# Two adjoining blocks on one core: the modulation chunks of the linear attention's input stage are computed behind its later projections, and the context and the small parameters are loaded later

## The reference, cut to what matters

```python
def modulate(h, shift, scale):
    return h * (1 + scale[:, None]) + shift[:, None]
...
    proj = h @ w_in
    q, k, v, g, a_lr = jnp.split(
        proj, [GLA_QK, 2 * GLA_QK, 2 * GLA_QK + GLA_VD, 2 * GLA_QK + 2 * GLA_VD], axis=-1)
    log_a = jax.nn.log_sigmoid((a_lr @ w_gate_up + b_gate).astype(jnp.float32)) / GLA_GATE_TAU
```

## Time and profile before

| | us |
|---|---|
| median of 3 runs | 1647.23 (1647.05 to 1648.43) |
| the profiled execution's own time | 1646.89 |
| span of its trace, first to last instruction | 1645.1 |
| PE busy (share of the span) | 1586.4 (96%) |
| DVE busy | 1025.4 (62%) |
| ACT busy | 650.4 (40%) |

### The profile page before, as it was taken

The page is one execution under the profiler, slowest core; times in us unless marked ns, Lnnn a source line. Parts: engine busy times, 40 slices in busy tenths (PEclk is TensorE's granted clock), DMA queues, the critical chain, the costliest instruction groups (busy, mean ns, idle before and its releaser), DMA issues.

```text
span 1645.1 us, 24028 instructions
## 1 busy us (share of the span) xinstructions
PE 1586.4 (96%) x9719; PEld 1235.1 (75%) x9719; DVE 1025.4 (62%) x1597; ACT 650.4 (40%) x925; POOL 0.2 (0%) x4
## 2 busy tenths in 40 slices
PE   6999899999999998999999999999999999999998
PEld 3788656766787875567677868977647788999998
DVE  3647654423795476454337968449857664689886
ACT  3444323322573442323236662424234342254443
POOL 0000000000000000000000000000000000000000
PEclk9999999999999998999999999999999999999999
DMA  9966798888998598888989973325622333645540
GB/s 350 304 227 218 259 358 339 335 322 329 360 346 279 188 317 325 306 342 311 349 327 359 342 235 101 104 77 204 229 79 79 105 124 119 214 137 197 179 155 26
DMA packets 188245, 393.12 MB, mean 239 GB/s; under 512 B 11365, under 2 KB 102232, under 8 KB 174824
## 3 DMA queue, kind: packets, MB, share of 16 engines
q1 hardware_dynamic: 186462, 390.21, 66.3%
q10 hardware_dynamic: 1674, 1.38, 0.3%
HBM read 390.52 MB, written 1.05 MB: 238 GB/s over the span
## 4 chain that ended last, share of the span: by engine, by line
PE 82%; DVE 8%; DMA 6%; ACT 2%; issue 1%; ACTq 0%; SPq 0%; DVEq 0%
PE bank L716 10%; PE bank L1129 8%; PE bank L1689 8%; PE bank L1156 4%; PE bank L1432 4%; PE bank L1192 4%; PE bank L1142 4%; PE bank L1700 4%; PE bank L1225 3%; PE bank L743 3%; PE bank L760 3%; DMA ring<-in_moe_w_up_dram 3%; PE bank L1210 2%; PE bank L807 2%; PE bank L776 2%; PE bank L911 2%
## 5 line engine op out<-in xcount | busy, mean ns | idle before, releaser
L2673 DVE TENSOR_TENSOR parts<-ring,parts 128x2048 fp32r<-128x2048 f32 x84 | 191.6, 2290 | 166.6 <-ACT parts L1998 166.0
L1787 ACT ACTIVATE work<-bank 128x256 f32<-128x256 f32 (+3 forms) x227 | 98.8, 447 | 378.1 <-PE bank L716 58.1
L1998 ACT ACTIVATE parts<-ring 128x2048 fp32r<-128x2048 f32 x84 | 160.5, 1921 | 150.9 <-DMA ring<-in_moe_w_up_dram 48.9
L716 PE MATMUL bank<-hh,ring 128*128 128x256 f32 x640 | 141.5, 380 | 2.3 <-ACT work L1787 1.8
L716 PEld LDWEIGHTS bank<-hh,ring 128*128 128x128 f32 x640 | 120.4, 190 | 21.6 <-issue 5.8
L1129 PE MATMUL bank<-parts 128*128 128x512 f32 x576 | 132.5, 391 | 0.0
L1689 PE MATMUL bank<-parts 128*128 128x256 f32 x1056 | 128.6, 283 | 1.4 <-DVE parts L3306 1.4
L1689 PEld LDWEIGHTS bank<-parts 128*128 128x128 f32 x1056 | 127.6, 192 | 2.2 <-issue 2.2
L1129 PEld LDWEIGHTS bank<-parts 128*128 128x128 f32 x576 | 107.7, 188 | 27.1 <-issue 4.9
L1156 PE MATMUL bank<-ring,work 128*64 128x512 f32 x512 | 113.6, 595 | 4.1 <-DMA ring<-in_moe_w_up_dram 4.1
L3262 DVE TENSOR_TENSOR parts<-ring,parts 128x2048 fp32r<-128x2048 f32 x37 | 84.8, 2292 | 16.2 <-ACT parts L2307 15.6
(11 more groups left out here) (379 smaller groups left out, 2709.6 us busy)
## 6 DMA issues: line engine op xcount, KB each, us to landing
ring<-in_moe_w_gate_dram SPq DMA_DIRECT2D x64, 1024.0 KB, 9.1
ring<-in_moe_w_up_dram SPq DMA_DIRECT2D x64, 1024.0 KB, 5.8
ring<-in_moe_w_down_dram SPq DMA_DIRECT2D x64, 1024.0 KB, 9.5
ring<-in_ada_w_dram SPq DMA_DIRECT2D x48, 1024.0 KB, 8.6
ring<-in_w_in_dram SPq DMA_DIRECT2D x32, 1024.0 KB, 5.9
ring<-in_w_mod_dram SPq DMA_DIRECT2D x24, 1024.0 KB, 7.5
ring<-in_w_up_dram SPq DMA_DIRECT2D x22, 1024.0 KB, 5.2
ring<-in_gla_w_in_dram SPq DMA_DIRECT2D x12, 1024.0 KB, 8.5
```

The costliest lines, as they stand in the source:

```text
L716: ins = pe.matmul(ps[:, 0:n], w[:, k, m * P:(m + 1) * P], rhs(k), start=k == 0, stop=k == kt - 1)
L1787: act.activation(dst, view, func, **kw).then_inc(tiles.taken, 1)
L1998: act.activation(moe_w[:, i % 3, 0, :], ring[:, g % RING, :], ACT.Identity)\
L2673: dve.tensor_tensor(moe_w[:, i % 3, 1, :], ring[:, (MOE_AT[layer] + AT[n, kind, half, 0]) % RING, :], moe_w[:, i % 3, 0, :].bitcast(F32), ...
```

## The change

Projections 0 to 3 are loaded and computed one behind the other; chunks 4 to 7 move behind projections 4, 5, 6 and 7. Chunks 4, 5 and 6 are turned behind projections 5, 6 and 7, chunk 7 behind projection 8. ACT's copies and DVE's reductions move with them. In SP's list slots 8 to 12 are projections 0 to 4, 13 and 14 chunk 4, 15 projection 5, 16 and 17 chunk 5, 18 projection 6, 19 and 20 chunk 6, 21 projection 7, 22 and 23 chunk 7, 24 projection 8; from 24 on the list is as before. The context is loaded ahead of slot 12, and the small parameters ahead of slots 13 to 24, four each.

```diff
--- before.py
+++ after.py
@@ -115,7 +115,7 @@
 MOD_CHUNKS = 12
 RING = 6
 FRONT = (2, 3, 0, 1)
-WITH_GLA_IN = {0: (0, 4), 1: (0, 5), 4: (0, 6), 5: (0, 7)}
+WITH_GLA_IN = {4: (0, 4), 5: (0, 5), 6: (0, 6), 7: (0, 7)}
 BEFORE_GLA_OUT = [(0, i) for i in range(8, 11)]
 WITH_ROUTER = [[(0, 11)] + [(1, i) for i in range(4)], [(1, 10), (1, 11)] + [(2, i) for i in range(4)]]
 SHARED = 8
@@ -635,7 +635,7 @@
             loads.append((d_skip[64 * (hd % 2):64 * (hd % 2) + 64, hd // 2:hd // 2 + 1],
                           A["s_d_2"][0, hd:hd + 1].rearrange("(n o) -> n o", o=1).to_broadcast([64, 1])))
         n_params = 16 * len(loads)
-        PARAMS_FROM, PARAMS_EACH = 9, 3
+        CTX_AT, PARAMS_FROM, PARAMS_EACH = 12, 13, 4

         def ring_half(n, b, of=ring):

@@ -936,24 +936,16 @@
                 ps = to_dve.fill(pe)
                 close(to_dve, pe.matmul(ps[:, 0:T], w_gate_up[:, m * P:(m + 1) * P], g_lr[0:16, :],
                                         start=True, stop=True))
-            mod_chunk(*WITH_GLA_IN[0])
-            in_linear(to_act, gla_parts)
-            mod_turn(4)
-            mod_chunk(*WITH_GLA_IN[1])
-            in_linear(to_act, gla_parts)
-            mod_turn(5)
-            in_linear(to_act, gla_parts)
+            for _ in range(3):
+                in_linear(to_act, gla_parts)
             pe.wait_ge(sem("ctx_landed"), 16)
             input_turned(c_in, "ctx_turned")
-            in_by_token(to_act, gla_parts)
-            mod_chunk(*WITH_GLA_IN[4])
-            in_by_token(to_act, gla_parts)
-            mod_turn(6)
-            mod_chunk(*WITH_GLA_IN[5])
-            in_by_token(to_act, gla_parts)
-            mod_turn(7)
-            in_by_token(to_act, gla_parts)
-            values_in = to_act.n
+            for j in range(4, 8):
+                in_by_token(to_act, gla_parts)
+                values_in = to_act.n
+                if j > 4:
+                    mod_turn(j - 1)
+                mod_chunk(*WITH_GLA_IN[j])
             pe.wait_ge(sem("gla_kdec"), 1)
             for t in range(TT):
                 ps = to_dve.fill(pe)
@@ -962,6 +954,7 @@
                 close(to_dve, ins)
             keys_in = to_dve.n
             in_linear(to_act, gla_parts)
+            mod_turn(7)
             norm_sum([sq[:, k, T:TC] for k in range(KT)], T)
             pe.wait_ge(to_dve.taken, keys_in)
             pe.wait_ge(to_act.taken, values_in)
@@ -1738,7 +1731,7 @@
             experts_at = {}
             sp.wait_ge(sem("cleared"), 1)
             for g, (what, arg) in enumerate(SLOTS):
-                if g == PARAMS_FROM - 1:
+                if g == CTX_AT:
                     sp.dma_start(c_in, A["ctx_2"][0].rearrange("(t p) n -> p t n", p=P)).then_inc(sem("ctx_landed"), 16)
                 at = PARAMS_EACH * max(g - PARAMS_FROM, 0)
                 for to, src in loads[at:at + PARAMS_EACH] if g >= PARAMS_FROM else ():
@@ -1920,7 +1913,6 @@
             for j in range(2):
                 take(g_q[:, j, :], scale=float(P) ** -0.5)
             in_high_halves(2)
-            take_mod()
             log_tables()
             act.wait_ge(sem("gla_neg"), 1)
             a(act.activation(g_l, g_l, ACT.Exp))
@@ -1940,8 +1931,7 @@
                 for t in range(TT):
                     take(g_v[:, t, j * 256:(j + 1) * 256])
                 in_high_halves(6 + j)
-                if j < 2:
-                    take_mod()
+                take_mod()
             act.wait_ge(sem("dve_tile_taken"), marks["ctx_turned", 3])
             act.activation(sq[:, :, T:TC], hh[:, :, 0:T], ACT.Square).then_inc(s["norm_sq"], 1)
             for j in range(2):
@@ -2482,7 +2472,6 @@
             stt(g_l, g_z, -1.0, g_z, mul, ALU.min, done=sem("gla_neg"))
             ts(g_z, g_z, 0.0, None, ALU.min)
             in_low_halves(2)
-            take_mod(*WITH_GLA_IN[0])
             dve.wait_ge(sem("gla_log"), 1)
             tt(g_z, g_z, g_l, sub)
             in_low_halves(3)
@@ -2496,7 +2485,6 @@
                 lc = g_l[:, j, :].rearrange("p (n t) -> p n t", n=CHUNKS)
                 tt(lc, lc, g_gam[:, j, :].unsqueeze(2).to_broadcast([P, CHUNKS, 64]), sub,
                    done=sem("gla_rest") if j == 3 else s["dve_step"])
-            take_mod(*WITH_GLA_IN[1])
             in_low_halves(5)
             input_turned(hh[:, :, 0:T])
             dve.wait_ge(sem("gla_decay"), 1)
@@ -2506,10 +2494,12 @@
             in_low_halves(7)
             take_mod(*WITH_GLA_IN[5])
             in_low_halves(8)
+            take_mod(*WITH_GLA_IN[6])
             for t in range(TT):
                 ps = take()
                 took(dve.tensor_copy(g_kt[:, t, :], ps))
             in_low_halves(9)
+            take_mod(*WITH_GLA_IN[7])
             for n in range(CHUNKS):
                 for pair in range(2):
                     ps = take()
```

## The result

The changed kernel takes 1654.43 us (median of 6 runs, 1651.25 to 1657.68), the kernel before 1647.59 (6 runs, 1647.05 to 1648.43): a ratio of 1.0041, 95% interval 1.0031 to 1.0051, or 5.1 to 8.4 us slower. The forecast was 1651.9 with 1645.0 to 1654.8. In a second measurement on another occasion the changed kernel took 1652.55 against 1647.42, 1.0029 (1.0020 to 1.0038). The profiled execution took 1653.74 us with a span of 1652.0.

What follows compares the result with a forecast made beforehand. PE, busy 96%, was taken as the bound, though loads may decide in the input stage: 4.4 us of stalls to win against a new 6.5 us wait; 4.7 us later, from 1646.89 to 1651.6, plus 0.3, 1651.9; range 1645.0 to 1654.8.

Steps and rivals of the forecast that it cites:

- case A: The forecast itself: a new 6.5 us wait of PE before chunk 5's turn, 4.7 us later, 1651.9 us; chance 0.50.
- The stall that stays: Turn of chunk 4: PE waits 1.1 us for ACT's copy, written behind the rounding of projection 6's weights.
- The new wait: Turn of chunk 5: PE waits 6.5 us for ACT's copy, queued behind projection 7's late weights.
- The clock: Behind the new wait the granted clock falls to 0.50; charged 1.5 us, ends 0 and 3.4.
- rival E: Up to 110 us as forecast, but the end doesn't move with it: 1647.2 to 1650 us; chance 0.05.
- B: Set of loads near line rate, 10.5 us; wait 2.2 us, too short for the clock; 1646.4 us; chance 0.27.
- C: No new wait, as DMA has room between 50 and 72 us; 1644.5 us, down to 1642.8; chance 0.10.
- The 0.60 us goes, and no more: PE's wait ahead of projection 0 for DVE's low half goes with the context's load; projection 0 starts at 38.5.
- I take 14.8: Parameters 24 to 35, chunk 6's two slots and projection 7: 14.8 us from projection 6's landing to 7's, range from 10.5.
- SP reaches slot 21 in time: Projection 7's load: its slot is free at projection 5's end, 79.6, and the queue has work until then.
- Just covered: Projection 8 lands at 101.5 behind chunk 7's slots; with rounding and copy chunk 6 is ready at 104.1.
- rival D: A runs worse: clock low for 6.8 us, 1.9 more, chunk 6's copy late by about 1 us; 1654.8; chance 0.08.

Runs made afterwards that it cites:

- copy first: The changed kernel with ACT's copy of a chunk written ahead of the rounding of projections 6 to 9: 1650.21 us, ratio 1.0015.
- set late: The changed kernel with parameters 26, 27, 29, 30 and 31 moved behind slot 25: 1648.91 us, ratio 1.0009.
- loads early: The changed kernel with eight parameters instead of four ahead of each slot from 13, all 48 out before slot 18: 1646.40 us, ratio 0.9991.

## Why the prediction was right

**The mechanism was case A**, step by step; the number is close to the upper end of the range, 0.4 us inside it, and in the second measurement 2.3. The front: projection 4 ended at 70.2 us (forecast 71.8), both stalls and the two chunks gone. The stall that stays: 0.62 us (forecast 1.1). The new wait: 7.69 us for ACT's copy, behind the rounding of projection 7, which landed at 92.15 (forecast 6.5, 92.8). The clock: 1.5 us on the turn and the chunk, as charged (2.2 in the second execution). The sums begin 6.4 us later than before instead of 4.7. From there to the end the changed kernel takes 1652.0 - 116.1 = 1535.9 us and the kernel before 1645.1 - 109.8 = 1535.3, so the shift went through; rival E falls. B and C fall with the 16.1 us between the two landings.

**Terms that were mis-sized.** "The 0.60 us goes, and no more" was too small: projection 0 began at 37.4 instead of 38.5, since in this execution the low-rank product ran at the full clock. That part is luck: in the second execution it ran at half and projection 0 began at 38.3. "I take 14.8" for the set, called the top of its range, was 16.1 and 15.4, above it both times; what in it was longer than in the kernel before, whose row it came from, no run shows. The sentence "SP reaches slot 21 in time" was wrong, 84.15 instead of 79.6, because of the hold-up at `lam_p`; what this cost by itself is not shown. "Just covered" for projection 8 was the largest miss in the other direction: `d_skip`'s eight loads took SP 6.3 us, slot 24 was issued at 93.99 and landed 10.0 us later, at 104.0 instead of 101.5, and PE waited 1.97 us at chunk 6's turn. I had that hold-up in rival D, at 1 us. Chunk 5's turn came 0.7 us earlier than forecast (94.71 against 95.4), the early front having outweighed the longer set, and the 1.97 us came on top: most of the 1.7 us between 4.7 and 6.4. The medians differ by 6.8. One sum of the forecast doesn't come out of its terms: for A's lower end, a wait of 5 us and a clock that costs nothing give 1649.2 and not 1649.7.

**The Trainium skill's figure** of 0.95 us for a 64 KB load ("DMA: Bandwidth & Descriptors", Bandwidth, Measured) gives 2.9 us for the three; taking them away won 2.7 to 3.4. The size agrees, but the page's row is for loads issued from GpSimd, and these are issued by SP, in rows of 64 bytes; no run here times one of them alone. The sum that I made of it, 12.9 us for the whole set, fell short, because the line rate of 390 GB/s for the rest was too good: without all five large and small members the rest, three loads of 1 MB and tiny ones, still took 10.2 us, where 390 GB/s gives 8.1.

**What stays open.** Whether the hole in the DMA rate is made where the packets are generated or where they are moved, no run separates. That the half clock goes with the wait, "copy first" bears out: chunk 5's turn and the matmuls behind it ran at the full clock, and the fall came behind the 4.39 us. How long a wait brings it is open: behind 1.84 us in "set late" the clock fell, behind the changed kernel's 1.97 us at chunk 6's turn it stayed.

## What to carry to other kernels

When work is moved behind other work on one engine, read the load list as well: what goes between two loads whose distance the engines can't cover decides, and a set that was harmless in one place (ratio 0.9998 with the old order of chunks) put 16.1 us between two loads in another, where 9.5 were left without it. Issue the many small loads while the queue has room (here 39 to 70 us), and look at each short copy that another engine waits for and that is written behind work that waits for a load. With the change the moves gave 1646.4 us (loads early), 1650.2 (copy first) and 1642.1 (both); in the kernel before the copy first won nothing.

## What the runs showed of the hardware

Windows of the low-rank product in two executions of the same program, the changed kernel, then PE idle around chunk 5 in the second:

```profile
31.90:38.70 6.80, 5.80 (x39) 3.73 (x39) 6.11 (x13) 6.47 (x13) 0.00 (x0) 1.00 1.10 349
```

```profile
31.90:38.50 6.60, 6.58 (x28) 3.49 (x27) 5.86 (x12) 4.63 (x9) 0.00 (x0) 0.50 1.10 349
89.90:100.00 10.10, 5.46 (x24) 2.16 (x25) 2.70 (x4) 3.03 (x5) 0.00 (x0) 0.50 0.86 295
```

The clock is granted in full in one and at half in the other, with the same program ahead of it; projection 0 began at 37.4 and at 38.3 us. Behind the long wait half the clock was granted for 6.7 us in the first (the window from 91.1 above) and for 10.1 in the second. So a single execution of this kernel is uncertain by about a microsecond from the clock in the low-rank product alone, and I had not expected the kernel before to spread from 1644.46 to 1651.78 us over later sessions when its first six runs lay within 1.4 us.
